# The last level of a blocked triangular inverse: from masked 128x128 products, one direction at a time, to 64x64 products on opposite quarters of the array

## The reference

```python
m = jnp.einsum('bhncd,bhnsd->bhncs', k_beta, k) * decay
m = jnp.where(tri_strict, m, 0.0) + jnp.eye(CHUNK, dtype=jnp.float32)
rhs = jnp.concatenate([v * beta[..., None], k_beta * jnp.exp(g)[..., None]], axis=-1)
sol = lax.linalg.triangular_solve(m, rhs, left_side=True, lower=True, unit_diagonal=True)
```

## Time and profile before

| | us |
|---|---|
| median of 3 runs | 2593.26 |
| lowest and highest | 2592.95, 2595.0 |
| the profiled execution | 2584.58 |
| its span, first to last instruction | 2582.8 |
| PE busy | 2337.6 (91%) |
| DVE busy | 1394.7 (54%) |
| ACT busy | 927.3 (36%) |

### The profile page before, as it was taken

The page is one execution under the profiler, slowest core; times in us unless marked ns, Lnnn a source line. Parts: engine busy times, 40 slices in busy tenths (PEclk is TensorE's granted clock), DMA queues, the critical chain, the costliest instruction groups (busy, mean ns, idle before and its releaser), DMA issues. The chain is left out here.

```text
span 2582.8 us, 40809 instructions
## 1 busy us (share of the span) xinstructions
PE 2337.6 (91%) x14870; PEld 1931.1 (75%) x14870; DVE 1394.7 (54%) x2377; ACT 927.3 (36%) x1727; POOL 136.8 (5%) x187
## 2 busy tenths in 40 slices
PE   6799898998989898998999878999999999999687
PEld 3278786877768686877778757788887878878686
DVE  1343655555454555555564354656566665766554
ACT  3433324242423324242422253433424244242423
POOL 0000000000001000000100020000000000000002
PEclk8899999999999999999999989999999999999898
DMA  8964434352434445252545415533434344343453
GB/s 321 353 188 130 111 107 126 89 134 78 123 100 124 110 110 131 73 149 73 168 121 160 147 57 156 127 102 96 128 83 120 91 108 113 96 122 92 129 154 105
DMA packets 553603, 329.72 MB, mean 128 GB/s; under 512 B 48658, under 2 KB 517814, under 8 KB 552710
## 3 DMA queue, kind: packets, MB, share of 16 engines
q1 hardware_dynamic: 393174, 218.59, 30.5%
q10 hardware_dynamic: 160240, 109.13, 14.4%
q0 software_dynamic: 64, 0.20, 0.0%
HBM read 304.73 MB, written 23.13 MB: 127 GB/s over the span
## 5 line engine op out<-in xcount | busy, mean ns | idle before, releaser
L1699 PE MATMUL ps<-h_hi,w_hi 128*128 128x512 f32 (+1 forms) x2080 | 825.9, 397 | 17.6 <-DVE w_lo L1060 7.6
L1700 PE MATMUL ps<-h_lo,w_hi 128*128 128x512 f32 (+1 forms) x2080 | 765.1, 368 | 0.0
L1701 PE MATMUL ps<-h_hi,w_lo 128*128 128x512 f32 (+1 forms) x2080 | 764.2, 367 | 0.0
L1060 DVE TENSOR_TENSOR w_lo<-w_raw,w_hi 128x1024 fp32r<-128x1024 f32 (+1 forms) x332 | 399.2, 1202 | 345.9 <-ACT w_hi L607 280.0
L607 ACT CAST w_hi<-w_raw 128x1024 fp32r<-128x1024 f32 (+1 forms) x332 | 341.8, 1030 | 441.0 <-PE ps L1701 142.4
L1699 PEld LDWEIGHTS ps<-h_hi,w_hi 128*128 128x128 f32 x2080 | 398.4, 192 | 110.0 <-issue 42.6
L1701 PEld LDWEIGHTS ps<-h_hi,w_lo 128*128 128x128 f32 x2080 | 396.3, 191 | 67.5
L1700 PEld LDWEIGHTS ps<-h_lo,w_hi 128*128 128x128 f32 x2080 | 398.8, 192 | 46.5
L1060 DVE TENSOR_TENSOR arena<-arena,ps 128x512 f32<-128x512 f32 (+1 forms) x192 | 117.6, 640 | 107.4 <-PE ps L1790 106.0
L1959 PE MATMUL ps<-h_hi,w_hi 128*128 128x512 f32 (+1 forms) x448 | 160.6, 359 | 15.5 <-ACT arena L773 10.6
L1780 PE MATMUL ps<-arena 128*128 128x128 f32 x768 | 110.4, 290 | 55.6 <-DVE arena L1312 55.6
(11 more groups left out here) (191 smaller groups left out, 2740.4 us busy)
## 6 DMA issues: line engine op xcount, KB each, us to landing
w_raw<-in_w_in SPq DMA_DIRECT2D x260, 512.0 KB, 4.1
ada_raw<-in_w_ada ACTq DMA_DIRECT2D x128, 512.0 KB, 5.1
w_raw<-in_w_out SPq DMA_DIRECT2D x64, 448.0 KB, 3.7
arena<-in_w_ada SPq DMA_DIRECT2D x27, 512.0 KB, 8.3
w_raw<-in_w_ada SPq DMA_DIRECT2D x19, 512.0 KB, 8.5
ada_raw<-in_w_ada SPq DMA_DIRECT2D x18, 512.0 KB, 8.3
arena<-decay_rows ACTq DMA_DIRECT2D x16, 512.0 KB, 5.7
x_channel_major<-arena ACTq DMA_DIRECT2D x1, 4096.0 KB, 17.5
```

What stands on the lines that cost most here:

```text
L1060: return V.tensor_tensor(o, a, b, op)
L1699: mm(o, w_hi[:, s, k], h_hi[:, kt, t0:], start=kt == 0, stop=False)
L1700: before_last = mm(o, w_hi[:, s, k], h_lo[:, kt, t0:], start=False, stop=False)
L1701: last = mm(o, w_lo[:, s, k], h_hi[:, kt, t0:], start=False, stop=kt == KT - 1)
```

## The change

The last level leaves the scheme above. The kernel keeps `times_m`, `mask_x`, `times_inv` and `merge` for levels 0 and 1, and does the last one for both directions together, in two slots instead of four: CORNERS is slot 30 in layer 0 and 34 in layer 1, and the slot behind it.
- `corner_times_m` (PE): for each chunk one 64x64 product for each direction. d = 0 contracts over partitions 0 to 63 and writes partitions 64 to 127 of bank G0; d = 1 the reverse. It waits for the merges of level 1 of both directions.
- `copy_corners` (DVE): one plain copy of 128 partitions x 4 chunks x 64 columns to prod.
- `corner_times_inv` (PE): again one 64x64 product for each chunk and direction, into bank G1.
- `merge_corners` (DVE): two operations on 64 partitions x 4 x 64 that write the negated product into the corner of inv_T, where zeros stood.

`v_mul` then waits for one semaphore instead of two. PE also increments a new semaphore, corners_begun, before each of its two groups; nobody waits for it.

```diff
--- before.py
+++ after.py
@@ -359,7 +359,7 @@
         x_masked = [sem(f"x_masked{d}") for d in range(2)]
         t_product = [sem(f"t_product{d}") for d in range(2)]
         t_merged = [sem(f"t_merged{d}") for d in range(2)]
-        q_decayed, ks_product, r_ready = sem("q_decayed"), sem("ks_product"), sem("r_ready")
+        corners_begun, q_decayed, ks_product, r_ready = sem("corners_begun"), sem("q_decayed"), sem("ks_product"), sem("r_ready")
         v_product, v_ready, s_product, s_ready = sem("v_product"), sem("v_ready"), sem("s_product"), sem("s_ready")
         ob_product, ob_squared, ob_summed, ob_rms, ob_normed = sem("ob_product"), sem("ob_squared"), sem("ob_summed"), sem("ob_rms"), sem("ob_normed")
         ob_turned, yb_ready, yb_stored = sem("ob_turned"), sem("yb_ready"), sem("yb_stored")
@@ -419,8 +419,12 @@
             return i * per + (HEADS * layer + off) * per + idx
 
         LVL = len(LEVELS)
+        LEVELS_OF = (LVL, LVL - 1)
+        WIDE = LEVELS[-1]
+        QUAD = (slice(0, WIDE), slice(WIDE, 2 * WIDE))
         TURN_BACK, GRAM = {0: 4, 1: 5}, {0: 6, 1: 7}
         SUBST, SOLVED, LEVEL0 = {0: 12, 1: 15}, {0: 20, 1: 24}, {0: 22, 1: 26}
+        CORNERS = {0: 30, 1: 34}
         V_SLOT = {0: (35, 41, 47, 53), 1: (39, 44, 49, 54)}
         O_SLOT = {0: 56, 1: 57}
         SCORE, TURN_P, ATTEND = {0: (3, 11, 19, 27), 1: (4, 16)}, {0: 5, 1: 6}, {0: 7, 1: 8}
@@ -1326,18 +1330,33 @@
                         vec.wait_ge(q_decayed, h())
 
                     def mask_x(d, n):
-                        vec.wait_ge(x_product[d], h(-1, LVL, n + 1))
+                        vec.wait_ge(x_product[d], h(-1, LEVELS_OF[d], n + 1))
                         tt(prod[:, d], quads(GX[d]), msk[:, n, d].unsqueeze(1).to_broadcast([P, NT, P]),
                            ALU.mult).then_inc(x_masked[d], 1)
-                        vec.wait_ge(x_masked[d], h(-1, LVL, n + 1))
+                        vec.wait_ge(x_masked[d], h(-1, LEVELS_OF[d], n + 1))
 
                     def merge(d, n):
-                        vec.wait_ge(t_product[d], h(-1, LVL, n + 1))
-                        if n < LVL - 1:
-                            own.go(tt(inv[:, d], inv[:, d], quads(GX[d]), ALU.subtract))
+                        vec.wait_ge(t_product[d], h(-1, LEVELS_OF[d], n + 1))
+                        own.go(tt(inv[:, d], inv[:, d], quads(GX[d]), ALU.subtract))
                         tt(inv_T[:, d], inv_T[:, d], quads(GT[d]), ALU.subtract).then_inc(t_merged[d], 1)
-                        vec.wait_ge(t_merged[d], h(-1, LVL, n + 1))
+                        vec.wait_ge(t_merged[d], h(-1, LEVELS_OF[d], n + 1))
                         own.settle()
+
+                    def copy_corners():
+
+                        vec.wait_ge(x_product[0], h(-1, LVL, LVL))
+                        V.tensor_copy(prod[:, 0, :, 0:WIDE], quads(G0)[:, :, 0:WIDE]).then_inc(x_masked[0], 1)
+                        vec.wait_ge(x_masked[0], h(-1, LVL, LVL))
+
+                    def merge_corners():
+                        vec.wait_ge(t_product[0], h(-1, LVL, LVL))
+                        for d in range(2):
+                            m = V.tensor_scalar(inv_T[QUAD[d], d, :, QUAD[1 - d]], quads(G1)[QUAD[d], :, 0:WIDE], -1.0, None, ALU.mult)
+                            if d == 0:
+                                own.go(m)
+                        m.then_inc(t_merged[0], 1)
+                        own.settle()
+                        vec.wait_ge(t_merged[0], h(-1, LVL, LVL))
 
                     def state(j):
                         vec.wait_ge(s_product, h(-1, 3, j + 1))
@@ -1466,11 +1485,13 @@
                             put(SUBST[layer] + n, substitute_backward, n)
                         put(SOLVED[layer], turn_inv, 0)
                         put(SOLVED[layer] + 1, turn_inv, 1)
-                        for n in range(LVL):
+                        for n in range(LVL - 1):
                             put(LEVEL0[layer] + 4 * n, mask_x, 0, n)
                             put(LEVEL0[layer] + 1 + 4 * n, mask_x, 1, n)
                             put(LEVEL0[layer] + 2 + 4 * n, merge, 0, n)
                             put(LEVEL0[layer] + 3 + 4 * n, merge, 1, n)
+                        put(CORNERS[layer], copy_corners)
+                        put(CORNERS[layer] + 1, merge_corners)
                         for j in range(3):
                             put(V_SLOT[layer][j] + 2, state, j)
                             put(V_SLOT[layer][j] + 3, residual, j + 1)
@@ -1775,20 +1796,39 @@
                         if n == 0:
                             pe.wait_ge(inv_turned, h(-1, 2, d + 1))
                         else:
-                            pe.wait_ge(t_merged[d], h(-1, LVL, n))
+                            pe.wait_ge(t_merged[d], h(-1, LEVELS_OF[d], n))
                         for cc in range(NT):
                             last = mm(quads(GX[d])[:, cc], m_T[:, d, cc], inv[:, d, cc], start=True, stop=True)
                         last.then_inc(x_product[d], 1)
 
                     def times_inv(d, n):
-                        pe.wait_ge(x_masked[d], h(-1, LVL, n + 1))
+                        pe.wait_ge(x_masked[d], h(-1, LEVELS_OF[d], n + 1))
                         if project and (d, n) == (0, 0):
                             pe.wait_ge(mod_ready, i * ADA_IN[layer] + (ada_before(layer) + ADA_EARLY[layer]))
                         for cc in range(NT):
-                            if n < LVL - 1:
-                                mm(quads(GX[d])[:, cc], inv_T[:, d, cc], prod[:, d, cc], start=True, stop=True)
+                            mm(quads(GX[d])[:, cc], inv_T[:, d, cc], prod[:, d, cc], start=True, stop=True)
                             last = mm(quads(GT[d])[:, cc], prod[:, d, cc], inv_T[:, d, cc], start=True, stop=True)
                         last.then_inc(t_product[d], 1)
+
+                    def corner_times_m():
+
+                        for d in range(2):
+                            pe.wait_ge(t_merged[d], h(-1, LEVELS_OF[d], LVL - 1))
+                        pe.sem_inc(corners_begun, 1)
+                        for cc in range(NT):
+                            for d in range(2):
+                                last = mm(quads(G0)[QUAD[1 - d], cc, 0:WIDE], m_T[QUAD[d], d, cc, QUAD[1 - d]],
+                                          inv[QUAD[d], d, cc, QUAD[d]], start=True, stop=True)
+                        last.then_inc(x_product[0], 1)
+
+                    def corner_times_inv():
+                        pe.wait_ge(x_masked[0], h(-1, LVL, LVL))
+                        pe.sem_inc(corners_begun, 1)
+                        for cc in range(NT):
+                            for d in range(2):
+                                last = mm(quads(G1)[QUAD[d], cc, 0:WIDE], prod[QUAD[1 - d], 0, cc, 0:WIDE],
+                                          inv_T[QUAD[1 - d], d, cc, QUAD[1 - d]], start=True, stop=True)
+                        last.then_inc(t_product[0], 1)
 
                     def ks_mul(j):
                         pe.wait_ge(s_ready, h(-1, 3, j))
@@ -1799,8 +1839,7 @@
 
                     def v_mul(j):
                         if j == 0:
-                            for d in range(2):
-                                pe.wait_ge(t_merged[d], h(-1, LVL, LVL))
+                            pe.wait_ge(t_merged[0], h(-1, LVL, LVL))
                         else:
                             pe.wait_ge(r_ready, h(-1, 3, j))
                         for d in range(2):
@@ -1914,11 +1953,13 @@
                         put(2, turn_v)
                         put(TURN_BACK[layer], turn_back)
                         put(GRAM[layer], gram)
-                        for n in range(LVL):
+                        for n in range(LVL - 1):
                             put(LEVEL0[layer] + 4 * n, times_m, 0, n)
                             put(LEVEL0[layer] + 1 + 4 * n, times_m, 1, n)
                             put(LEVEL0[layer] + 2 + 4 * n, times_inv, 0, n)
                             put(LEVEL0[layer] + 3 + 4 * n, times_inv, 1, n)
+                        put(CORNERS[layer], corner_times_m)
+                        put(CORNERS[layer] + 1, corner_times_inv)
                         for j in range(4):
                             put(V_SLOT[layer][j], v_mul, j)
                             if j < 3:
```

## The result

| us | before | changed |
|---|---|---|
| median of five runs each | 2592.95 | 2576.28 |
| lowest and highest | 2588.78, 2595.0 | 2574.13, 2582.45 |
| the profiled execution | 2584.58 | 2574.13 |
| its span | 2582.8 | 2572.0 |

The ratio is 0.9944, with a 95% interval of 0.9927 to 0.9962: 0.6% faster, 16.7 us by the medians. The forecast was 2575.0. The two profiled executions differ by only 10.8 us in span; the first experiment shows where the rest comes from.

A forecast was written before the change was run, and what follows sets the result against it. PE, 91% busy, was taken as the bound, at the last level by its own instructions. Layer 1's 12.9 us, layer 0's 3.2 and the ninth bodies' 2.2 sum to 18.3, so 2593.3 becomes 2575.0 us, range 2568 to 2588.

The forecast's parts named there:

- The group, 0.78 us: PE, last level: eight products of 64 columns, 8 x 0.11 / 2, plus 0.34 for the mode; an old group costs 0.89.
- Two at a time: PE's new groups: products on opposite quarters of the array overlap in pairs, 0.78 us a group; chance 0.6 as summed.
- the rival's pace: One at a time: opposite quarters do not overlap, perhaps because they share a PSUM bank; 1.22 us a group, 2585.6; chance 0.22.
- The sign I gave for it: PE trace of the new groups: 0.6 to 0.7 us to the next projection, pairs of records almost at one time.
- the cost goes with the columns: From products of 128 columns (0.22 us) and 256 (0.43): a product of 64 should take 0.11 by itself.
- Layer 1, 1.84 us a body: Seven bodies: first group loses 0.05, second gains 1.89 without a wait; net 1.84 a body, 12.9 us for seven.
- Layer 0, 0.46 us a body: Seven bodies: PE idles 1.5 us for the copy, which takes most of the saving; gain 0.46 each, 3.2 in all.
- the second group starts at 476.38: Layer 0: copy ends at 476.33, group starts 0.05 later; it then takes 0.69, its entry hidden by the wait.
- The ninth bodies, 2.2: The two ninth bodies, with output projections of other lengths: 1.1 us gain each, bounds 0 and 1.84.
- Sum 18.3: Whole kernel: gains of 12.9, 3.2 and 2.2 us, taken from the median of 2593.3 to give 2575.0.
- Given back: Rival: the bodies gain, but a later wait that does not hang on PE's progress takes it; 2593 us; chance 0.07.
- The increment of corners_begun, nothing: PE's sequencer, before each group: taken at no cost; bound 0.39 in seven layer 1 bodies, 2.7 us in all.

The follow-up runs named there:

- the first experiment: Both kernels run again without any edit: the changed kernel 2576.72 us, ratio 0.9954; the kernel before, one more execution, 2592.77 us.
- the three kernels in which the wait was 0.42 us or less: Layer 1's turn_p and attention steps one slot later: with both groups late 2553.79 us, in the kernel before 2580.41, in the changed kernel 2565.84.

## Why the prediction was right

**The group, 0.78 us.** Entered 0.09 to 0.10 late (PE's step ahead of it is 0.33 instead of 0.23, where it doesn't wait), 0.61 to the next projection, and 0.11 for the step after that (0.34): 0.81. Two at a time was right: the rival's pace appears when the order of the products is changed, and its bank is no matter. The sign I gave for it, records of a pair almost at one time, shows in 9 of the 32 groups only; in the others two streams of records interleave, 36 and 22 ns apart, and the group is as long. The reason I gave for 0.11 us a product was wrong. I had it from "the cost goes with the columns", read from moving columns; a product of 64 moving columns on the whole array costs 0.22 like one of 128. The quarter is cheap since its stationary tile has 64 columns. Both readings give the same number here, and a different one for the first group on the whole array.

**Layer 1, 1.84 us a body.** Measured 1.80. The second group has no wait, as forecast; the first starts 0.10 us behind the merge by its records (1794.37 to 1794.46), where the steps had 0.05.

**Layer 0, 0.46 us a body.** Measured 0.33. DVE's order and the copy were right to 0.01 us, and the wait was right too: forecast as 1.5 from start to start, it measures 1.51 so (473.71 + 0.23 to 475.45); the bracket's 1.34 leaves out the recorded length of the matmul ahead. The term that was off is "the second group starts at 476.38", 0.05 behind the copy, "its entry hidden by the wait": the copy ends at 475.30 and the group starts at 475.45, 0.15 behind. What the extra 0.10 is made of stays open. The first group starts 0.10 behind its merge, and just so in the kernel that has it on the whole array, where other products start 0.055 behind what they wait for (L1801, L1837): half of the extra can arise without quarters. The group with the step behind it, 0.61 + 0.11 against the 0.69 of the sum, adds the other 0.03.

**The ninth bodies, 2.2.** Measured 0.87 + 1.64 = 2.5.

**Sum 18.3.** The local intervals lose 17.7. In the time 16.7 arrive by the medians. "Given back" was a rival with a price of all of it; it takes place in small: 3.2 us in layer 1, of which 2.3 come back where the half clock is gone on both sides. I had named no part for the clock, and the forecast of body periods (1.8 shorter) holds only for the bodies without half clock, 108.95 to 106.97. That the median came out within 1.3 us of 2575.0 is luck in part: the ratio's interval reaches from 9.8 to 18.9 us of gain, and the clock's share, which I had left out, is larger than that 1.3 (4.6 us in layer 1 alone).

**The increment of corners_begun, nothing.** The kernel with the first group on the whole array settles it for the two ninth bodies, where no wait precedes the group: the increment is issued, and the group starts 0.228 and 0.121 us behind the product before it, the plain steps there being 0.227 and 0.120. In the changed kernel the same two places have 0.318 and 0.209. So the 0.09 belongs to the quarters, as for the strips of `ada_multiply`. Behind a wait the increment isn't separated.

## What to carry to other kernels

A small product costs what its stationary tile's columns cost to load, so cut the stationary side, and put neighbours in program order on opposite parts of the array: the same eight products in another order lost most of the gain, half of it through their own pace and the rest with the clock. When a stage is made shorter, count the slots between producer and consumer again, since what covered the copy may have been the work that was removed: one slot more was worth 8 us, where the change itself had brought 17. And read where the clock falls: a wait of 2 us can cost 1.5 us more at half clock behind it, in some rounds of a loop and not in others.

## What the runs showed of the hardware

- The half clock behind one and the same wait of 2.1 to 2.3 us came in 1 of the 7 projecting bodies of layer 1 in the kernel before (my expectations speak of eight; seven is right), in 4 and 5 in the changed one, in 5 in each of the four kernels with two banks, with the first group on the whole array, with the second group late and with both late, in all 7 when the directions went in turn, and in none of the 21 bodies of the three kernels in which the wait was 0.42 us or less. What picks the bodies stays open: the period doesn't by itself, with one of seven at 108.95 us and all seven at 109.1. The Trainium skill (TensorE: Matmul & The Clock Gate, HAM oscillation — how this bites in real kernels) tells of a longer wait, for DMA, in a loop that throttles the array anew in every round; here a wait for DVE did so in some rounds, and in every one only in the run with directions in turn.
- fp32 records on one quarter stand 58 ns apart, two on opposite quarters 58 ns a pair, records with a 128-column stationary tile 112 ns whether 64 or 128 columns move.
- Going to 64x64 tiles costs 0.09 to 0.10 us ahead of the group where PE doesn't wait, and the step behind it is 0.11 too long, where a whole-array f32 group has 0.08. A direction's first step in the group is 77 or 107 ns instead of 58.
